# Mixing of values in three reduced-precision passes, two softmax divisions moved ahead of a weight split, and the convolution's first tap on GpSimd

## The reference, cut to what matters

```
z = h @ w_in[i]
q, k, v, xr, yr, ga, gr = split(z)                 # 8 query heads, 2 key/value heads of 128
q, k = partial_rope(q), partial_rope(k)
logits = q @ k.T * 128**-0.5                       # where |i - j| <= 128, else -1e30
probs = softmax([logits, sink])[..., :-1]          # a learned sink logit per head
attn = probs @ v                                   # "mixing of values"
for direction in (forward, backward):
    y = sum(w[k] * shifted(xr, k) for k in range(4)) + b     # depthwise convolution of width 4
    gates = sigmoid(y @ w_a + b_a), sigmoid(y @ w_x + b_x)   # 4 blocks of 256 x 256
    hr += scan(decay(gate_a), y * gate_x * sqrt(1 - decay**2))
rnn = hr * gelu(yr)
m = sigmoid(ga) * (attn @ w_proj_attn) + sigmoid(gr) * (rnn @ w_proj_rnn)
h = layer_norm(alpha * h + m @ w_out)
h = layer_norm(alpha * h + mlp(h) + per_layer_embedding(h, p))
```

## Time and profile before

| What | us |
|---|---|
| median of three executions | 949.04 |
| the profiled execution | 949.1 |
| its span, first to last instruction | 947.3 |
| PE busy in the span | 927.0 (98%) |
| DVE busy | 729.6 (77%) |
| ACT busy | 577.1 (61%) |
| POOL busy | 1.4 |
| granted clock of TensorE, mean share of full speed | 0.997 |

### The profile page before, as it was taken

The page is one execution under the profiler, slowest core; times in us unless marked ns, Lnnn a source line. Parts: engine busy times, 40 slices in busy tenths (PEclk is TensorE's granted clock), DMA queues, the critical chain, the costliest instruction groups (busy, mean ns, idle before and its releaser), DMA issues.

```text
span 947.3 us, 12574 instructions
## 1 busy us (share of the span) xinstructions
PE 927.0 (98%) x5100; PEld 800.1 (84%) x5100; DVE 729.6 (77%) x981; ACT 577.1 (61%) x730; POOL 1.4 (0%) x9
## 2 busy tenths in 40 slices
PE   5999999999999999999999999999999999999996
PEld 3898988988888888888889889888888888888885
DVE  5888898787867867767868698888878676866755
ACT  4578899764356644555345889987435564545540
POOL 0000000000000000000000000000000000000000
PEclk9999999999999999999999999999999999999998
DMA  9546444584485555566443644456656656555521
GB/s 333 153 163 200 136 156 157 185 305 164 156 266 182 199 198 178 192 203 204 160 161 119 211 159 155 134 180 197 256 179 217 226 187 205 186 180 198 201 89 45
DMA packets 118457, 174.62 MB, mean 184 GB/s; under 512 B 3968, under 2 KB 78976, under 8 KB 117888
## 3 DMA queue, kind: packets, MB, share of 16 engines
q1 hardware_dynamic: 118256, 173.79, 55.0%
q10 hardware_dynamic: 144, 0.03, 0.0%
HBM read 172.76 MB, written 1.05 MB: 183 GB/s over the span
## 4 chain that ended last, share of the span: by engine, by line
PE 88%; DVE 7%; ACT 4%; DMA 0%; issue 0%; DVEq 0%; ACTq 0%
PE ring L548 13%; PE ring L550 13%; PE ring L549 13%; PE ring L601 9%; PE ring L597 9%; PE misc L548 5%; PE misc L549 5%; PE misc L550 5%; PE ring L600 5%; PE ring L598 5%; PE misc L778 2%; DVE sb_w_lo L1253 2%; PE ring L721 1%; PE misc L837 1%; ACT sb_w_hi L933 1%; DVE sb_tmp L1485 1%
## 5 line engine op out<-in xcount | busy, mean ns | idle before, releaser
L1253 DVE TENSOR_TENSOR sb_w_lo<-sb_raw,sb_w_hi 128x2048 fp32r<-128x2048 f32 x138 | 294.8, 2148 | 65.8 <-ACT sb_w_hi L933 65.8
L933 ACT CAST sb_w_hi<-sb_raw 128x2048 fp32r<-128x2048 f32 x138 | 246.3, 1796 | 19.6 <-DMA sb_raw<-in_w_out_dram 4.3
L601 PE MATMUL ring<-sb_x_both,sb_w_hi 128*128 128x512 f32 x272 | 107.6, 396 | 0.0
L597 PE MATMUL ring<-sb_x_both,sb_w_hi 128*128 128x512 f32 x272 | 107.5, 395 | 0.0
L548 PE MATMUL ring<-sb_w_hi,sb_x_both 128*128 128x512 f32 x272 | 107.1, 394 | 0.0
L549 PE MATMUL ring<-sb_w_lo,sb_x_both 128*128 128x512 f32 x272 | 106.0, 390 | 0.0
L550 PE MATMUL ring<-sb_w_hi,sb_x_both 128*128 128x512 f32 x272 | 106.0, 390 | 0.0
L600 PE MATMUL ring<-sb_x_both,sb_w_lo 128*128 128x256 f32 x272 | 75.7, 278 | 0.0
L598 PE MATMUL ring<-sb_x_both,sb_w_lo 128*128 128x256 f32 x272 | 75.4, 277 | 0.0
L548 PE MATMUL ring<-sb_x_both,sb_w_hi 128*128 128x256 f32 x256 | 72.6, 284 | 0.0
L550 PE MATMUL ring<-sb_x_both,sb_w_lo 128*128 128x256 f32 x256 | 72.4, 283 | 0.0
(11 more groups left out here) (229 smaller groups left out, 2111.8 us busy)
## 6 DMA issues: line engine op xcount, KB each, us to landing
sb_raw<-in_w_in_dram SPq DMA_DIRECT2D x40, 1024.0 KB, 5.3
sb_raw<-in_w_up_dram SPq DMA_DIRECT2D x34, 1024.0 KB, 5.2
sb_raw<-in_w_down_dram SPq DMA_DIRECT2D x18, 1024.0 KB, 5.0
sb_raw<-in_w_proj_attn_dram SPq DMA_DIRECT2D x8, 1024.0 KB, 5.2
sb_raw<-in_w_proj_rnn_dram SPq DMA_DIRECT2D x8, 1024.0 KB, 5.1
sb_hb<-in_w_up_dram SPq DMA_DIRECT2D x8, 1024.0 KB, 5.3
sb_raw<-in_w_out_dram SPq DMA_DIRECT2D x6, 1024.0 KB, 6.2
sb_raw<-in_w_ple_gate_dram SPq DMA_DIRECT2D x6, 1024.0 KB, 5.4
```

The source lines that it names most:

```text
L597: nc.tensor.matmul(bank_of(*key), hi[:, cols], x_both[:, k], start=k == 0, stop=False)
L601: last = nc.tensor.matmul(bank_of(*key), hi[:, cols], x_both[:, k + 1], start=False, stop=k + 2 == KT)
L933: nc.scalar.copy(hi_at[home][:, at], raw_at[home][:, at]).then_inc(s_hi_part, 1)
L1253: nc.vector.tensor_tensor(lo_at[home][:, 0:size], raw_at[home][:, 0:size], hi_at[home][:, 0:size].bitcast(F32), ALU.subtract).then_inc(s_s ...
```

## The change

1. `mix_values` calls `three` for each of the two key blocks: six F32R matmuls of 128x512 in place of two float32 ones. It takes high and low parts of the values (`v_hi`, `v_lo`) and of the turned probabilities (`p_hi`, `p_lo`).
2. `probs_back` on ACT now writes `p_hi` in place of `pT`, and stands ahead of `split_to(l, name, 1)` where it stood behind it. `probs_low` on DVE is new: p_lo from PSUM less p_hi, 128x1024, four times a layer, behind `gate_input` and ahead of `split_to(l, name, 1)`. `v_hi` (ACT, behind the last copy of q and k in block 2) and `v_low` (DVE, block 3) are new, 128x512, once a layer. The four new tiles lie in memory of tiles that are free by then.
3. `softmax_norm` of rounds 1 and 3 (blocks 4 and 6) goes ahead of `split_to(l, name, 0)` on DVE; those of rounds 0 and 2 stay behind it.
4. `conv_base` leaves ACT and runs on POOL as `tensor_scalar` (multiply, add), two of 128x256 per block, 32 in all, each with its own semaphore step. They stand alone in POOL's stream, with the same waits as before on ACT.

```diff
+        qk, at = sb_at("qk", [P, TT, QK_HEADS, HEAD_DIM])
+        v_hi = again("v_hi", [P, TT, KV_HEADS, HEAD_DIM], F32R, at + 4 * KT * SEQ)
+        v, at = sb_at("v", [P, TT, KV_HEADS, HEAD_DIM])
+        v_lo = again("v_lo", [P, TT, KV_HEADS, HEAD_DIM], F32R, at)
+        qkT, at = sb_at("qkT", [P, QK_HEADS, SEQ], F32R)
+        p_lo = again("p_lo", [P, TT, GROUP, P], F32R, at)
...
+            def conv_base(l, i):
+
+                direction, b = divmod(i, RNN_BLOCKS)
+                if i == 0:
+                    pool.wait_ge(s_small, 32 * l + 32)
+                xr = (l, f"xr{b // 2}", b % 2)
+                pool.wait_ge(s_emptied[RING[xr][0]], read_out(*xr))
+                pool.wait_ge(s_gated, value("gated", l, max(0, i - 1)))
+                for j in range(2):
+                    ft = 2 * b + j
+                    nc.gpsimd.tensor_scalar(xc[:, i % 2, j, :], xT[:, ft, :], rnnp[:, direction, ft, 0:1],
+                                            rnnp[:, direction, ft, 4:5], ALU.mult, ALU.add).then_inc(s_conv_base, 1)
+
+            for l in range(DEPTH):
+                for i in range(2 * RNN_BLOCKS):
+                    conv_base(l, i)
...
             def mix_values(l, r):
 
-                pe.wait_ge(s_probs_back, value("probs_back", l, r + 1))
+                pe.wait_ge(s_v_ready, value("v_ready", l, 1))
+                pe.wait_ge(s_probs_lo, value("probs_lo", l, r + 1))
                 for kb in range(TT):
-                    last = nc.tensor.matmul(misc[:, 2, :], v[:, kb, r // TT, :], pT[:, kb, :, :],
-                                            start=kb == 0, stop=kb == TT - 1)
+                    last = three(misc[:, 2, :], [x[:, kb, r // TT, :] for x in (v_hi, v_lo)],
+                                 [p_hi[:, kb, :, :], p_lo[:, kb, :, :]], kb == 0, kb == TT - 1)
                 last.then_inc(s_mixed, 1)
...
             def probs_back(l, r):
                 act.wait_ge(s_probs_turned, value("probs_turned", l, r + 1))
-                nc.scalar.copy(pT[:, :, :, :].rearrange("p a g t -> p (a g t)"),
+                nc.scalar.copy(p_hi[:, :, :, :].rearrange("p a g t -> p (a g t)"),
                                misc[:, 2:4, :].rearrange("p a n -> p (a n)")).then_inc(s_probs_back, 1)
...
                 unit_out(l, "q1")
                 split_to(l, "xr0", 0)
                 xr_out(l, 0, 0)
-                conv_base(l, 0)
                 split_to(l, "xr0", 1)
                 xr_out(l, 0, 1)
                 conv_hi(l, 0)
-                conv_base(l, 1)
                 split_to(l, "xr1", 0)
                 xr_out(l, 1, 0)
                 conv_hi(l, 1)
@@ -1153,7 +1162,6 @@
                 gate_curves(l, 0)
                 split_to(l, "xr1", 1)
                 xr_out(l, 1, 1)
-                conv_base(l, 2)
                 for i, name in enumerate(WITH_BLOCK[1:], 1):
                     split_to(l, name, 0)
                     if i >= 4:
@@ -1166,15 +1174,16 @@
                     if name == "ga0":
                         qk_copies(l, range(4))
                     gate_curves(l, i)
+                    if 3 <= i <= 6:
+                        probs_back(l, i - 3)
                     split_to(l, name, 1)
                     if name == "kv":
                         unit_out(l, name)
-                    if i + 2 < 2 * RNN_BLOCKS:
-                        conv_base(l, i + 2)
                     if name == "ga0":
                         qk_copies(l, [4])
-                    if 3 <= i <= 6:
-                        probs_back(l, i - 3)
+                        all_emptied(act, l, [("kv", t) for t in range(TT)])
+                        nc.scalar.copy(v_hi[:, :, :, :].rearrange("p t h d -> p (t h d)"),
+                                       v[:, :, :, :].rearrange("p t h d -> p (t h d)")).then_inc(s_v_hi, 1)
                     if i % 2 == 1:
                         root(l, i // 2)
                     if name == "gr0":
...
+            def v_low(l):
+                dve.wait_ge(s_v_hi, value("v_hi", l, 1))
+                nc.vector.tensor_tensor(v_lo[:, :, :, :].rearrange("p t h d -> p (t h d)"),
+                                        v[:, :, :, :].rearrange("p t h d -> p (t h d)"),
+                                        v_hi[:, :, :, :].rearrange("p t h d -> p (t h d)").bitcast(F32),
+                                        ALU.subtract).then_inc(s_v_ready, 1)
+
+            def probs_low(l, r):
+
+                dve.wait_ge(s_probs_back, value("probs_back", l, r + 1))
+                if r == 0:
+                    dve.wait_ge(s_scores, value("scores", l, TT))
+                nc.vector.tensor_tensor(p_lo[:, :, :, :].rearrange("p a g t -> p (a g t)"),
+                                        misc[:, 2:4, :].rearrange("p a n -> p (a n)"),
+                                        p_hi[:, :, :, :].rearrange("p a g t -> p (a g t)").bitcast(F32),
+                                        ALU.subtract).then_inc(s_probs_lo, 1)
+
...
-                dve.wait_ge(s_conv_base, value("conv_base", l, i + 1))
+                dve.wait_ge(s_conv_base, value("conv_base", l, 2 * i + 2))
...
                 split_to(l, "xr1", 1)
                 conv(l, 2)
                 for i, name in enumerate(WITH_BLOCK[1:], 1):
+                    if i in (4, 6):
+                        softmax_norm(l, i - 3)
                     split_to(l, name, 0)
-                    if 3 <= i <= 6:
+                    if i in (3, 5):
                         softmax_norm(l, i - 3)
                     if i >= 4:
                         attn_out(l, i - 4)
@@ -1646,6 +1674,10 @@
                         conv_lo(l, i + 1)
                     split_to(l, f"rg{i // RNN_BLOCKS}", i % RNN_BLOCKS)
                     gate_input(l, i)
+                    if i == 3:
+                        v_low(l)
+                    if 3 <= i <= 6:
+                        probs_low(l, i - 3)
                     split_to(l, name, 1)
                     if i + 2 < 2 * RNN_BLOCKS:
                         conv(l, i + 2)
```

More of the change, by code:

```diff
@@ L238 @@
 PER = dict(
-    qk_lo_ready=5, ln_step=2 * TT * LN_STEPS, ln_norm=4 * TT, x_turned=3 * 4, x_hi=3 * 4, x_ready=3 * 4,
+    qk_lo_ready=5, probs_lo=ROUNDS, v_ready=1, v_hi=1, ln_step=2 * TT * LN_STEPS, ln_norm=4 * TT, x_turned=3 * 4, x_hi=3 * 4, x_ready=3 * 4,
     rope_step=6, qk_turned=5, qk_ready=5,
@@ L242 @@
     probs_back=ROUNDS, mixed=ROUNDS, attn_hi=ROUNDS, attn_ready=ROUNDS,
-    param_step=16, param_exp=1, conv_base=8, conv_step=48, rin_hi=8, rin_ready=8,
+    param_step=16, param_exp=1, conv_base=16, conv_step=48, rin_hi=8, rin_ready=8,
     decay=16, pair_ready=8, m2_done=8, gated=8, root=GROUPS, rg_step=3 * GROUPS, scanned=GROUPS,
@@ L284, in hybrid_encoder @@
         lnp = sb("lnp", [P, 2, D])
-        qk = sb("qk", [P, TT, QK_HEADS, HEAD_DIM])
-        v = sb("v", [P, TT, KV_HEADS, HEAD_DIM])
-        qkT = sb("qkT", [P, QK_HEADS, SEQ], F32R)
+        qk, at = sb_at("qk", [P, TT, QK_HEADS, HEAD_DIM])
[4 more added lines that the diff above has]
+        p_lo = again("p_lo", [P, TT, GROUP, P], F32R, at)
         yg = qk[:, :, :, :].rearrange("p t h d -> p (t h d)")[:, 0:KT * SEQ].rearrange(
@@ L296, in hybrid_encoder @@
         soft = sb("soft", [P, GROUP, SEQ])
-        pT = sb("pT", [P, TT, GROUP, P])
+        pT, at = sb_at("pT", [P, TT, GROUP, P])
+        p_hi = again("p_hi", [P, TT, GROUP, P], F32R, at)
         scan_in, at = sb_at("scan_in", [P, 2, 4, SEQ])
@@ L354, in hybrid_encoder @@
         s_probs_back = sem("probs_back")
+        s_probs_lo = sem("probs_lo")
+        s_v_hi = sem("v_hi")
+        s_v_ready = sem("v_ready")
         s_mixed = sem("mixed")
@@ L959, in out_of @@
                 nc.scalar.activation(dst, bank_of(*key), func, scale=scale).then_inc(s_emptied[RING[key][0]], 1)
-            def conv_base(l, i):
-                direction, b = divmod(i, RNN_BLOCKS)
-                if i == 0:
-                    act.wait_ge(s_small, 32 * l + 32)
-                xr = (l, f"xr{b // 2}", b % 2)
-                act.wait_ge(s_emptied[RING[xr][0]], read_out(*xr))
-                act.wait_ge(s_gated, value("gated", l, max(0, i - 1)))
-                for j in range(2):
-                    ft = 2 * b + j
-                    last = nc.scalar.activation(xc[:, i % 2, j, :], xT[:, ft, :], ACT.Identity,
-                                                bias=rnnp[:, direction, ft, 4:5], scale=rnnp[:, direction, ft, 0:1])
-                last.then_inc(s_conv_base, 1)
             def conv_hi(l, i):
```

## The result

The changed kernel took 954.04 us (median of 6; before 949.02, of 6): ratio 1.0052, 95% interval 1.004 to 1.0064, so slower, by more than a measurement is uncertain. 951.6 was forecast. The upper end of the range was 954.0, which the median passes by 0.04, so the range holds only to the tenth in which it was stated. Of the profiled execution (954.09) the span, from first to last instruction, has 952.0, and 2.1 lie outside it; before it was 947.3 and 1.8. Of the 5.0 us more, 4.36 are there when PE's last matmul starts (943.64 against 939.28), 0.3 lie behind that in the span, and 0.3 outside.

The account below looks back on a forecast made before the run. PE was taken as the bound, busy 927.0 of 947.3 us. Its savings were outweighed by later waits on DVE's attn_out: two layers at +1.23 us, +2.5 on 949.1, gave 951.6; the 8-in-10 range was 947.5 to 954.0.

Parts of the forecast that it names:

- Part 1: Mixing on PE: six F32R matmuls take 1.36 us instead of 1.71, sparing 0.35 a round.
- Part 2: Block 4, gate product: without conv_base on ACT, PE's wait on ga1 goes, 0.58 us, twice in the kernel.
- Part 3: Transposes of round 1: the later cast delays DVE's split 0.90 us and attn_out to 129.44; PE starts near 129.6.
- Part 4: Same delay through rounds 1 and 2: splits 1.58 and 2.71 us later, round 3's transposes 1.58; a layer 1.23 longer.
- What costs nothing: Low parts of weights, v_hi, probs_low of rounds 1 to 3 and conv_base on POOL (0.8 us for two) delay nothing.
- The sum: Whole kernel: two layers at +1.23 us are +2.5, on 949.1 giving 951.6.
- POOL holds DVE up: Block 2: POOL and DVE exclude each other, delaying split or convolution; +0.9 us a layer, 953.4 in all; chance 0.25.
- Moved division: Block 4 on DVE: division and split change places, but attn_out stands behind both in either order; gain nil.
- all gain: Rival: DVE's and ACT's changes disappear in idle time, attn_out keeps its 0.20 us; 3.9 us go, 945.2; chance 0.12.
- One wait only: Rival: ACT catches up in block 5 and round 3 is ready in time; -0.2 us a layer, 948.7; chance 0.15.
- main case: Two waits of PE on attn_out in each layer, before transposes of rounds 1 and 3; 951.6 us, chance 0.40.

Follow-up runs that it names:

- e6: Changed kernel with block 4's first tap (conv_base) alone back on ACT, the other seven on POOL: 952.17 us, ratio 1.0031.
- e2: Changed kernel with POOL's tensor_scalar replaced by a memset that reads nothing (convolution results wrong): 953.10 us, ratio 1.0039.
- e1: Changed kernel with all first taps (conv_base) back on ACT at their old places: 951.90 us, ratio 1.0028.
- e3: Changed kernel with DVE's attn_out ahead of the split in blocks 4 and 6: 951.77 us, ratio 1.003.
- e4: Kernel before with only conv_base moved from ACT to POOL: 951.63 us, ratio 1.0028.
- e5: Kernel before with only the softmax divisions of rounds 1 and 3 moved ahead of the split: 949.79 us, ratio 1.0009.
- e9: Kernel before with seven of the eight first taps (conv_base) on POOL and block 4's on ACT as before: 949.34 us, ratio 1.0002.
- e10: Changed kernel with block 4's first tap on ACT and attn_out ahead of the split in blocks 4 and 6: 949.31 us, ratio 1.0003.

## Why the prediction was right in kind and short in size

*Part 1, mixing in 1.36 us:* right, 1.39 by the distances in block 4.

*Part 2, the wait on ga1 goes:* wrong, 0.69. ACT lost the 1.09 us of `conv_base` as forecast, but its exponentials of round 0 started at 105.20 where they were at 104.34, since DVE's softmax was behind the late convolution; the two nearly cancel. ACT by time (answers the earlier trace rows):

```profile
112.69 1.00 ACT L1049 CAST sb_p_hi<-misc 128x1024 fp32r<-128x1024 f32 x1
113.58 1.91 ACT L958 CAST sb_w_hi<-sb_raw 128x2048 fp32r<-128x2048 f32 x1
...
119.18 0.60 ACT L984 ACTIVATE sb_ga<-ring 128x512 f32<-128x512 f32 x1
```

Without the hold it goes (e6, e2). It doesn't matter for the end either way, as part 3 had said of PE's lead: e6 has no such wait and e1 one of 0.76, and their layers are equally long.

*Part 3, the transposes of round 1 at 129.6:* right without POOL (129.46 in e1), 0.9 short with it (130.47). The wait was forecast near 1.7 and is 1.70, but that is luck: PE comes 0.8 later than I had it (near 128.63, which is 119.92 and the 8.71 that the kernel before takes from there; 127.86 was forecast), and DVE 0.9 later. A wait that fits proves less than the two times on either side of it.

*Part 4:* forecast 1.58 for the split of block 4, 2.71 for block 5 and 1.58 for the transposes of round 3; measured 2.48, 3.58 and 2.44. Each is 0.9 over, which is the hold of block 2 handed through. In e1, where there is none, the transposes of round 3 are 1.44 late, or 1.6 behind its start, which was 0.17 early. The chain was right. The wait in front of them was forecast near 1.2 and is 0.94; a gap of 0.22 ahead of gr0, which the forecast did not have, stands before it.

*What costs nothing:* here is the step that failed. The sum put `conv_base` on POOL at nothing, and it costs 2.5 us of the 5.0 (e1 against the changed kernel): 0.92 a layer and 0.6 at the end. Its length was not the error. I took 0.8 us for two, within 0.6 to 1.2, and it is 1.09, which the ACT form (1.09) had shown. The error was to let two engines work side by side in block 2 that don't. "POOL holds DVE up" was a rival with 0.25 and 0.9 us a layer, and that is what happened. It named the block and, as one of two possibilities, the late convolution. DVE's split isn't longer (2.31); POOL's first instruction is held until it ends. But that the price fits is luck: the rival had twice 0.4 and a hand-over of 0.1 behind the split, and measured are 0.27 for the rest of the first instruction, 0.55 for the second and 0.04. The rival's 953.4 lacks 0.3 us outside the span, which the kernels with taps on POOL show (1.90 to 2.23 against 1.77 to 1.84 for the four without), and 0.3 behind PE's last matmul. The latter only those four have in which POOL works for all eight blocks (after, e2, e3, e4: 8.25 to 8.36 from there to the end of the span, the others 7.98 to 8.11). Why both are longer stays open.

*Moved division:* I wrote that both orders are the same in front of the write-out. In the changed kernel they are; by itself the move costs 0.32 of idle DVE (e5).

The rival *all gain* is out, since it needs the write-out of round 0 in time, and that is late in every altered kernel but those that move it ahead of the split. *One wait only* is out, since it needs round 3 ready in time, and PE waits 0.94 there (0.93 in e1, without POOL's hold).

The kind of the forecast, slower by two waits on the write-out in each layer, was right for its reasons. The main case alone spanned 950.6 to 952.6. It is the rival that stretched the range to 954.0 and so to the measured time.

## What to carry to other kernels

When a chain on one engine is dense up to something that the bounding engine waits for, a gain anywhere else ends as a longer wait there (e6, e9), and a wait taken away there ends at the next consumer of the same engine (e3, e10). Look for the engine's idle gaps instead, and for moves that fill them; here two moves on DVE were worth 1.94 us a layer together, 4.3 by the medians. And a step that is put on an idle engine has to be laid against what the others read at that moment, instruction by instruction: one pair of eight cost 0.93 us a layer (e6 against the changed kernel), and the other seven cost TensorE nothing in the blocks.

## What the hardware showed

- A GpSimd tensor_scalar that reads SBUF does not run beside a VectorE instruction with two SBUF inputs. In the changed kernel its first instruction of block 2 is on record for 2.96 us against 0.56 for the one at 60.73, and it ends 0.3 after the split. Wherever GpSimd came second it lost; the split kept its 2.29 to 2.31 us. In block 2 it did not get in between two VectorE instructions either: its record starts at 96.31, under VectorE's 0.69 us instruction and ahead of the split at 96.70, and yet the split ran first.
- Where GpSimd's instruction was already running, VectorE lost, if little. In block 5 of the changed kernel GpSimd's second instruction runs until 149.22 and VectorE's begins at 148.99. It has 0.77 on record (0.76 to 0.78 in every kernel with this tap on GpSimd), where it has 0.69 before, and 0.69 in e2 with the memset. GpSimd, VectorE, and VectorE before:

```profile
148.13 1.09 POOL L560 TENSOR_SCALAR sb_tmp<-sb_xT,sb_rnnp 128x256 f32<-128x256 f32 x2 [13.90 <-DVE sb_hb L1527]
```

```profile
148.99 0.77 DVE L1531 SCALAR_TENSOR_TENSOR sb_scan_in<-sb_tmp,sb_scan_in 128x512 f32<-128x512 f32 x1 [1.04 <-ACT sb_tmp L1027]
```

```profile
146.53 0.69 DVE L1505 SCALAR_TENSOR_TENSOR sb_scan_in<-sb_tmp,sb_scan_in 128x512 f32<-128x512 f32 x1 [1.06 <-ACT sb_tmp L1016]
```

- A VectorE subtraction with one input in PSUM (`probs_low`) holds GpSimd for nothing: 1.40 for the pair in block 4, where 0.3 of waiting for `gate_input` and 1.09 make 1.40. A GpSimd memset, which only writes, is not held either (0.57 the pair). The Trainium skill, "SBUF — State Buffer", section "Who interferes with whom", says both, and the trace agrees. The same section says that the order of issue, and not the shape of an instruction, decides who is blocked; the trace agrees in that either engine can be the one that waits (0.77 against 0.69 above). It does not where GpSimd is already waiting: there its record starts 0.39 ahead of the split's, and the split still went first.
- The first tap, 128x256 of float32 with a multiply and an add, takes GpSimd 0.55 us (1.09 the pair), the same as ScalarE (1.09 the pair).
